# One layer of a conformer and mLSTM hybrid on one core: the order of a head's small matrix products, updates and copies is changed

## What is computed

```python
u = u_a * sigmoid(u_g)
c = conv_general_dilated(concat(conv_buf, u), w_dw, ...) + b_dw      # 31 taps, depthwise
# mLSTM, for each head, chunk by chunk
s = einsum('bthk,bshk->btsh', qc, kc) * w_intra
num = einsum('btsh,bshv->bthv', s, vc) + w_inter * einsum('bhvk,bthk->bthv', C, qc)
den = sum(s, axis=2) + w_inter * einsum('bhk,bthk->bth', n, qc)
h = num / maximum(abs(den), exp(-m_t))
C_new = dec * C + einsum('bsh,bshv,bshk->bhvk', wk, vc, kc)
n_new = dec * n + einsum('bsh,bshk->bhk', wk, kc)
hm = h * rsqrt(mean(h * h) + EPS) * g_mh * sigmoid(o)
```

## Time and profile before

| | us |
|---|---|
| median of 3 runs | 1351.9 (1348.71 to 1354.8) |
| the profiled execution: its own time | 1349.91 |
| its span in the profile | 1348.2 |
| TensorE busy (matmul) | 1272.1, 94% |
| TensorE weight loads (beside the matmuls) | 1184.2, 88% |
| VectorE busy | 734.4, 54% |
| ScalarE busy | 485.3, 36% |
| GpSimd busy | 81.6, 6% |
| mean granted TensorE clock | 0.976 |

### The profile page before, as it was taken

How to read it: one execution, slowest core, us unless ns; L and a number is a source line. 1 busy time by engine, 2 the same in 40 slices (tenths; PEclk the granted TensorE clock), 3 DMA queues, 4 the chain that set the end, 5 groups by cost and what they waited for, 6 DMA issues and landing times.

```text
span 1348.2 us, 23801 instructions
## 1 busy us (share of the span) xinstructions
PE 1272.1 (94%) x9123; PEld 1184.2 (88%) x9123; DVE 734.4 (54%) x994; ACT 485.3 (36%) x701; POOL 81.6 (6%) x139
## 2 busy tenths in 40 slices
PE   6999998999899899989999999995999999999994
PEld 5999967987697688669999999994999999999993
DVE  4343688787888877785455533435644212444324
ACT  6333531452344145314574322235433212333111
POOL 3011101101100110010000000002000000000002
PEclk8999999999999999999999999997999999999997
DMA  5235725505441541341322222330222222222211
GB/s 185 79 117 157 100 88 179 182 31 183 154 141 47 186 182 62 124 156 49 110 79 94 87 86 93 124 114 16 79 93 79 94 93 78 94 78 94 94 47 66
DMA packets 39777, 141.31 MB, mean 105 GB/s; under 512 B 5012, under 2 KB 5524, under 8 KB 39592
## 3 DMA queue, kind: packets, MB, share of 16 engines
q1 hardware_dynamic: 27848, 99.37, 23.0%
q0 software_dynamic: 11872, 41.23, 9.1%
HBM read 118.31 MB, written 22.26 MB: 104 GB/s over the span
## 4 chain that ended last, share of the span: by engine, by line
PE 81%; DVE 8%; issue 6%; ACT 2%; DMA 1%; DVEq 1%; POOL 0%; ACTq 0%; POOLq 0%; SPq 0%
PE product L1254 78%; PE side L1254 3%; DVE accp L962 3%; DVE y L1198 1%; DMA wraw<-in_wstream 1%; DVE wlo L811 1%; DVE crg L1068 1%; DVE accs L975 0%; ACT L667 0%; DMA x<-in_xT 0%; ACT fr L518 0%; DVE pt L1059 0%; ACT L529 0%; DVEq L961 0%; PE side L1391 0%
## 5 line engine op out<-in xcount | busy, mean ns | idle before, releaser
L1254 PE MATMUL product<-ahi,whi 128*128 128x256 f32 (+1 forms) x1536 | 325.0, 293 | 19.0 <-DVE alo L836 10.8
L811 DVE TENSOR_TENSOR wlo<-wraw,whi 128x1024 fp32r<-128x1024 f32 x176 | 214.8, 1223 | 232.4 <-ACT whi L510 224.1
L1254 PE MATMUL product<-ahi,wlo 128*128 128x256 f32 (+1 forms) x1536 | 321.5, 291 | 0.0
L1254 PE MATMUL product<-alo,whi 128*128 128x256 f32 (+1 forms) x1536 | 319.6, 290 | 0.0
L1254 PEld LDWEIGHTS product<-ahi,whi 128*128 128x128 f32 x1536 | 250.4, 192 | 24.2 <-issue 21.5
L510 ACT ACTIVATE whi<-wraw 128x1024 fp32r<-128x1024 f32 x176 | 185.0, 1052 | 240.1 <-PE product L1254 163.0
L1254 PEld LDWEIGHTS product<-alo,whi 128*128 128x128 f32 x1536 | 250.2, 192 | 0.0
L1254 PEld LDWEIGHTS product<-ahi,wlo 128*128 128x128 f32 x1536 | 249.2, 191 | 0.0
L962 DVE SCALAR_TENSOR_TENSOR accp<-u,wdw,accp 128x512 f32<-128x512 f32 x240 | 163.4, 745 | 0.5
L1254 PE MATMUL product<-hidhi,wlo 128*128 128x256 f32 (+1 forms) x512 | 105.8, 287 | 0.0
L1254 PE MATMUL product<-hidlo,whi 128*128 128x256 f32 (+1 forms) x512 | 105.7, 288 | 0.0
(11 more groups left out here) (249 smaller groups left out, 1638.6 us busy)
## 6 DMA issues: line engine op xcount, KB each, us to landing
wraw<-in_wstream SPq DMA_DIRECT2D x176, 512.0 KB, 3.4
crg<-in_c_in POOLq DMA_DIRECT2D x32, 512.0 KB, 6.1
out_c_s<-crg POOLq DMA_DIRECT2D x32, 512.0 KB, 2.9
hb<-head_rows POOLq DMA_DIRECT2D x4, 580.0 KB, 5.6
x<-in_xT SPq DMA_DIRECT2D x4, 544.0 KB, 5.4
sgm<-in_xT SPq DMA_DIRECT2D x1, 2176.0 KB, 9.1
out_yT<-y SPq DMA_DIRECT2D x8, 272.0 KB, 2.1
out_c_p<-cst POOLq DMA_DIRECT2D x4, 512.0 KB, 6.8
```

The costliest lines, as they stand in the source:

```text
L811: V.tensor_tensor(wlo[:, k % RING, :, :], wraw[:, k % 2, :, :], whi[:, k % RING, :, :].bitcast(f32), ALU.subtract).then_inc(lo_done, 1)
L1254: return pe.matmul(out, lhsT, rhs, start=start, stop=stop, skip_group_check=check)
```

## The change

- TensorE: the scores stand behind v2; the denominators (prompt and sample) stand behind v4, ahead of o0; `readout(0)`, cu0 and cu1 behind o0, and the sample's numerator behind them, so that the readout's first matmul starts the accumulation; the sums for n stand behind cu3; the transposes of the sample rows stand behind cc01.
- DVE: the products of the score weights stand behind the drain of v3; the maximum of the denominator stands behind `split(9)`; in the loop over the output gates the state updates and reciprocals stand ahead of the taps; some taps stand among the pv drains (`PV_TAPS`); it no longer computes `kws`, `hs` (twice) and the copies of the convolution into `u`.
- ACT: `kws`, the two rescalings of `hs` and the copies into `u` are added; the sigmoid of a gate chunk stands ahead of the copy of the next weights (`split(11 + k)`); a table for the sigmoid is loaded ahead of o0, and one set for logarithm and exponential behind o3.

```diff
-V_TAPS = [(5, 8), (8, 11), (11, 13), (13, 15)]
-O_TAPS = [(17, 18), (18, 20), (20, 24), (24, 27)]
+V_TAPS = [(5, 8), (8, 11), (11, 13), (13, 13)]
+O_TAPS = [(16, 18), (18, 18), (18, 21), (21, 24)]
+PV_TAPS = [(24, 24), (24, 26), (26, 26), (26, 28)]
...
+                act.wait_ge(bv_in, 16 * h + 16)
+                s = use("kts")
+                act.activation(kws[:, :], psum[s][0:NS, 0, 0:DK], ACT.Copy, scale=wkcol[:, bass.ds(h, 1)]).then_inc(drained[s], 1)
                 was_drained("kts")
...
                 for k in range(VT):
-                    split(11 + k)
+                    if k == 0:
+                        act.activation(warm[:, :], eps[:, :], ACT.Sigmoid).then_inc(table_in, 1)
                     s = use(f"o{k}")
                     act.activation(tile(hm, 4 * h + k), slot(s), ACT.Sigmoid, bias=c("b_o", 4 * h + k)).then_inc(drained[s], 1)
+                    split(11 + k)
+
+                act.preload_act_table_set("natural_log_exp_and_others")
+                act.wait_ge(snum_ready, h + 1)
+                act.wait_ge(srec_ready, h + 1)
+                apart(act)
+                act.activation(hs[:, :], side[:, 3, :], ACT.Copy, scale=sst[:, 1:2]).then_inc(hs_ready, 1)
...
+                act.wait_ge(hs_std, h + 1)
+                act.activation(hs[:, :], hs[:, :], ACT.Copy, scale=sst[:, 4:5]).then_inc(hs_norm, 1)
...
+                act.wait_ge(conv_saved, 16 * 2 * KT)
+                act.wait_ge(conv_sum, 2 * h + 2)
+                apart(act)
+                for q in range(2):
+                    act.activation(tile(u, 2 * h + q, 0, SEQ), accp[:, q:q + 1, :], ACT.Copy).then_inc(conv_copied, 1)
+                    act.activation(tile(u, 2 * h + q, SEQ, NS), accs[:, q:q + 1, :], ACT.Identity, bias=c("b_dw", 2 * h + q)).then_inc(conv_copied, 1)
...
                 for k in range(VT):
                     split(11 + k)
...
                     if k < 2:
                         update(2 * k)
                         update(2 * k + 1)
-                    taps(*O_TAPS[k])
                     if k == 1:
                         dve.wait_ge(dve_step, sd)
+                        V.reciprocal(sst[:, 1:2], sst[:, 0:1]).then_inc(srec_ready, 1)
+                        dve.wait_ge(dve_step, rd)
                         rd = mark(V.reciprocal(rden[:, :], rden[:, :]))
-                        sd = mark(V.reciprocal(sst[:, 1:2], sst[:, 0:1]))
-                dve.wait_ge(snum_ready, h + 1)
-                dve.wait_ge(dve_step, sd)
-                V.tensor_scalar(hs[:, :], side[:, 3, :], sst[:, 1:2], None, ALU.mult).then_inc(hs_ready, 1)
+                    taps(*O_TAPS[k])
...
+                    taps(*PV_TAPS[k])
+                taps(28, WIDTH - 1)
+                taps(WIDTH - 1, WIDTH)
```

More of the change, by code:

```diff
@@ L680, in state_out @@
                                    ACT.Copy).then_inc(drained[s], 1)
+                act.wait_ge(np_ready, h + 1)
+                act.activation(npn[:, bass.ds(h, 1), :], side[:, 2:3, P:P + QT], ACT.Copy).then_inc(np_used, 1)
                 for k in range(VT):
@@ L1033, in _ @@
                     if s_ == 0:
-                        s = use("kts")
-                        V.tensor_scalar(kws[:, :], psum[s][0:NS, 0, 0:DK], wkcol[:, hh], None, ALU.mult).then_inc(drained[s], 1)
                         dve.wait_ge(kh_ready, h + 1)
                         V.tensor_tensor(kwl[:, :], kws[:, :], kwh[:, :].bitcast(f32), ALU.subtract).then_inc(kl_ready, 1)
+                    if s_ == 3:
+                        dve.wait_ge(st_ready, 5 * h + 5)
+                        for q in range(ST + 1):
+                            dve.wait_ge(w_ready, 8 * h + ST + q)
+                            bank, at_ = ST_AT[q]
+                            if q < ST:
+                                w_ = SEQ - P * q
+                                d = pt[:, PT_AT[q]:PT_AT[q] + w_]
+                                V.tensor_tensor(d, d, side[:, bank, at_:at_ + w_], ALU.mult).then_inc(pt_ready, 1)
+                            else:
+                                d = spread(pts[:, :])
+                                V.tensor_tensor(d, d, by_quad(side[0:NS, bank, at_:at_ + NS]), ALU.mult).then_inc(pt_ready, 1)
                     if s_ < 2:
@@ L1049, in _ @@
                 V.tensor_tensor(vst[NS:2 * NS, :], vtok[0:NS, ST, :], vst[0:NS, :].bitcast(f32), ALU.subtract).then_inc(ops_ready, 1)
[L1050 to L1062, removed]
-                split(9)
+                split(9)
+                taps(13, 14)
+                dve.wait_ge(den_abs, h + 1)
+                dve.wait_ge(expm_ready, h + 1)
+                rd = mark(V.tensor_tensor(rden[:, :], rden[:, :], hb[:, R_M:R_M + SEQ], ALU.max))
+                dve.wait_ge(sden_abs, h + 1)
+                sd = mark(V.tensor_tensor(sst[:, 0:1], sst[:, 0:1], mcol[:, hh], ALU.max))
+                taps(14, 16)
                 split(10)
@@ L1368, in values, with scores @@
                     return ins
+                def scores():
+                    pe.wait_ge(kt_used, ST * h + ST)
+                    apart(pe)
+                    for q in range(ST + 1):
+                        bank, at_ = ST_AT[q]
+                        n_, w_ = (P, SEQ - P * q) if q < ST else (NS, NS)
+                        for kk in range(QT):
+                            ins = mm(side[0:n_, bank, at_:at_ + w_], kT[:, kk, P * q:P * q + n_], qT[:, kk, P * q:P * q + w_],
+                                     kk == 0, kk == QT - 1)
+                        ins.then_inc(st_ready, 1)
                 s = use("v0")
@@ new lines, in _ @@
+                for q in range(ST):
+                    ins = mm(side[:, 0, P * q:SEQ], ones[:, :], pt[:, PT_AT[q]:PT_AT[q] + SEQ - P * q], q == 0, q == ST - 1)
+                ins.then_inc(den_ready, 1)
+                pe.wait_ge(ops_ready, 5 * h + 4)
+                mm(side[:, 2, 0:1], pts[:, :], ones[0:NS, 0:1], True, False)
+                for kk in range(QT):
+                    ins = mm(side[:, 2, 0:1], qn[:, kk, :], ones[:, 0:1], False, kk == QT - 1)
+                ins.then_inc(sden_ready, 1)
@@ new lines, in _ @@
+                chunk("o0", 8)
+                readout(0)
+                pe.wait_ge(ops_ready, 5 * h + 5)
+                pe.wait_ge(vs_all, h + 1)
+                pe.wait_ge(kst_ready, 3 * DEC_B * (h + 1))
+                outer(0)
+                outer(1)
+                mm(side[:, 3, :], pts[:, :], vtok[0:NS, ST, :], False, False)
+                chunk("o1", 9)
+                outer(2)
+                outer(3)
+                pe.wait_ge(sden_abs, h + 1)
+                for kk in range(QT):
+                    for q in range(ST):
+                        ins = mm(side[:, 2, P + kk:P + kk + 1], kw[:, q, P * kk:P * (kk + 1)], ones[:, 0:1], q == 0, q == ST - 1)
@@ L1471, in _ @@
+                ins.then_inc(np_ready, 1)
+                chunk("o2", 10)
+                chunk("o3", 11)
                 readout(1).then_inc(snum_ready, 1)
@@ L1494, in _ @@
                 ins.then_inc(hst_ready, 1)
+                outer(6)
+                weighted(2)
+                outer(7)
+                weighted(3)
+                new_state(1)
+                pe.wait_ge(hsum_ready, 3 * h + 3)
+                mm(side[:, 1, :], ones[:, :], sqacc[:, :], True, True).then_inc(ss_ready, 1)
             def alternate(i, k, c0, s0, xhi, xlo, arrive=None):
```

91 lines of the change are left out of this document (21 added, 70 removed).

## The result

The changed kernel takes 1370.0 us (median of 4 runs, 1366.04 to 1374.84) against 1353.4 (1348.71 to 1355.39) of the kernel before: ratio 1.013, 95% interval 1.0084 to 1.0175. It is slower, and outside the range of the prediction. The profiled execution took 1366.04, 16.1 more than that of before (1349.91).

What follows compares the result with a forecast made beforehand. TensorE, busy 94% of the span, was taken as the bound. Waits of +1.35 and clock of -1.5 us a head gave -0.6 over four heads: 1349.3 profiled, 1351.3 from the median 1351.9; range 1346 to 1357, with rivals 1342 to 1360.

Steps and rivals of the forecast that it cites:

- Scores +1.3: Before the scores, now behind v2: a new TensorE wait of 1.3 us a head for ACT's kw.
- o0 +0.85: Before o0: a new wait of 0.85 us a head for DVE's chain behind v3, ending in the weight subtraction.
- cu1 -0.5: Before cu1: its wait goes, as cu0 and the readout lie between; 0.5 us a head saved.
- o1 -1.2, no half clock behind it: Before o1: 0.6 to 0.7 of the 1.84 us wait is left, 1.2 saved, and full clock behind it.
- o2 +0.9, behind ACT's late copy: Before o2: a stall of 1.0 where it had 0.1, as ACT copies the weights after o1's sigmoid.
- 1.27 stays: Before the second readout: the 1.27 us wait for its state loads stays unchanged.
- the stall at cu5 stays too: Before cu5: the 2.35 us wait for DVE to drain cu4 stays, changing by zero.
- The clock, -1.5 a head: Behind cu1, in o1: the half-clock stretch goes, saving 1.5 us a head, bounded at 0 to -1.5.
- Idle time: Over a head: TensorE idle 8 to 9 us instead of 7.
- hs, the conv copies, the sample rows: nothing: Work moved to ACT and later sample-row transposes cost zero; the conv copies have 1.2 us of cover at q0.
- The rival that came true: Smaller but more stalls, at cu3 and o2 and at cu5, bring six more half-clock stretches: +9, 1360.3 us; chance 12%.
- The fourth rival: At cu4: relieved DVE comes sooner, the 2.35 us stall goes with its clock stretches, 1338.9 us; chance 7%.

Runs made afterwards that it cites:

- e9: Kernel before with only ACT's order in the gate steps swapped, sigmoid ahead of the copy of the next weights: 1372.3 us, ratio 1.0133.
- e5: Changed kernel with ACT's gate-step order as before, copy of the next weights ahead of the sigmoid: 1333.3 us, ratio 0.9855.
- e10: Changed kernel with DVE's state updates ahead of the weight subtraction and the sums for n back between pv3 and cc23: 1346.1 us, ratio 0.9946.
- e4: Kernel before with one convolution tap moved from ahead of the updates of cu2 and cu3 to ahead of cu4's: 1361.6 us, ratio 1.0058.
- e6: Kernel before with convolution taps moved from ahead of the updates of cu4 to ahead of those of cu2 and cu3: 1339.8 us, ratio 0.9905.
- e1: Changed kernel with DVE's state updates put ahead of the weight subtraction of each gate step: 1357.2 us, ratio 1.0015.
- e2: Changed kernel with three convolution taps moved from ahead of the update of cu4 to behind the drain of v2: 1342.7 us, ratio 0.992.
- e7: Changed kernel with the scores behind v3 instead of v2: 1358.7 us, ratio 1.0032.
- e3: Changed kernel with DVE's updates ahead of the weight subtraction and three taps moved behind the drain of v2: 1330.7 us, ratio 0.9834.
- e11: Changed kernel with updates ahead of the subtraction, scores behind v3, DVE's sample sums ahead of its score products, some taps earlier: 1322.2 us, ratio 0.9767.

## Why the prediction was wrong, point by point

- **Scores +1.3, o0 +0.85.** Measured 1.23 and 0.63. Right.
- **cu1 -0.5.** Its wait is gone. Right.
- **o1 -1.2, no half clock behind it.** 0.63 is left in three heads, as foretold, and 1.15 in the first; the stretch behind cu1 is gone in those three and has stayed in the first. Right but for the first head, as a local statement.
- **o2 +0.9, behind ACT's late copy.** Measured 0.98 in place of 0.1, with DVE waiting 4.46 for the copy as the step said. e9 and e5 show the cause by adding and removing just that order. Right.
- **"1.27 stays", "the stall at cu5 stays too".** Their sum was right (3.62 foretold, 3.70 measured), the two terms were not. o2 ran at half clock, so its end came 1.6 us later (its sigmoid starts at 348.30, where 340.27, 6.1 for a chunk at full clock and 0.3 to hand over make 346.7), while the loads came no later: the load wait went. In e10, where o2 runs at full clock in every head, each head has a load wait again. The update of cu4 is tied to o3's end by sigmoid, copy, subtraction, six taps; TensorE reached cu5 that much sooner, and the two waits became one of 3.70. The prediction had the coupling only the other way round. Its zero for this part of the head is right all the same, in idle time: 8.13 us from o3's sigmoid to cu5 before, 8.14 after.
- **The clock, -1.5 a head.** This is the step that failed. I took away the stretch behind o1 and left all others where they were, by the size of the single stall. The trace of before already spoke against going by size: the readout of its first head waits 2.12 us, longer than the 1.83 of o1, and the clock stays at its upper level behind it.

```profile
222.06 1.92 PE L1254 MATMUL side<-crg,qm 128*32 128x512 f32 x16 [2.12 <-DMA crg<-in_c_in]
...
222.00:226.00 4.00, 3.94 (x23) 1.00 0.40 130
```

  After the change the stretch that was to be saved came back behind o2 in every head, and the merged stall before cu5 brought one or two in every head instead of two in all: 13 instead of the two that the sum implies. 11 stretches at 1.43 are 15.7 us, most of the 18.7 by which the forecast was low; one of them stands behind the wait in the first head told of below, and is not the change's. From the profiled execution, 1349.3, the forecast was 16.7 low.
- **Idle time.** 8.3 us in the second head, foretold 8 to 9. Over the heads the sum asked for 4 x 1.35 = 5.4 more; measured 9.2 more, 2.6 of it a wait that the profiled execution of before lacks (below).
- **hs, the conv copies, the sample rows: nothing.** No wait of TensorE is put down to them, and DVE's busy time fell from 734.4 to 724.9. e5 bounds them together: the change with ACT's old order is faster than before by 20 us (10.7 from profile to profile). The table load ahead of `hs` takes 1.28 and the next ACTIVATE starts 0.01 behind it, as the earlier trace rows had it. The Trainium skill, "ScalarE: Activation LUTs", "What ACT_TABLE_LOAD costs", counts a drain of about 1.38 us more; this trace shows none either.
- **The rival that came true** is the first one, with its own sign: "It decides if o2 runs at half clock", and "half clock behind cu3 in most heads" stood among the signs of being wrong. It gave 1360.3 and was still too low, since it added six stretches to a sum that had already taken four away. Its chance of 12% rested on a 1.27 us stall that had brought none, and in the kernel after 0.54 and 0.98 with the sums between them did.
- **The fourth rival**, DVE sooner at cu4, was kept down for "the weights' copy behind o3's sigmoid". e5 takes this copy away from there and gets it: the reason was the right one, and it says that the same edit which I priced at +0.9 a head cost the 9 a head (37 / 4; 27 / 4, near 7, from profile to profile) by which e5 is faster. The rival's 1338.9 for the whole is near e5's 1333.3 and 1339.2.

Two of the signs of being wrong came: half clock behind cu3 in all four heads, and heads longer than 123.5 us (124.0 to 127.0 between the first K transposes of one head and of the next). The time by the table: idle +9.2 and seven stretches, 10.0, make 19.2, and 3.1 less in the rest; measured 16.1. What stays open is which stalls bring half clock.

## What to carry to other kernels

Where one engine copies and another works behind that copy in order, the place of the copy in the first one's queue sets all that is queued in the second: ask not only who waits for the copy, but what stands behind the one who waits, here two updates and six taps that TensorE needed. Of two waits that hang on one chain, don't carry the sizes over: fix the chain's end, then see when the waiting engine gets there; a slower TensorE ahead of that end costs nothing, as e10's readout shows. And when stalls become smaller but stay, don't book the clock as won: count where the stretches at half clock were, price them from the rows, and keep their return as a rival of real weight.

## What the runs showed of the hardware

- A stretch at half clock cost 1.30 to 1.43 us of TensorE's busy time on average, with 14 to 30 of them a program. It costs no time where TensorE would have waited anyway (e10's readout).
- No size of a stall separates those with half clock from those without. The 1.83 before o1 brought it in every head of before, but the same wait of 1.83 or 1.84 at the same place in three heads of e4 and in two of e6 only. The 2.14 before e10's readout did, the 2.12 in the first head of before and the 2.50 in the first head of e6, both before the readout, didn't, nor did the 1.27. The 0.54 before cu3 with the one-column sums behind it brought it in every head of after, e1, e2 and e7 (in all of them but e1 a wait before o2 follows), in three heads of e5, and in one each of e3 and e11.
- In the first head TensorE waits 1.5 to 4.0 us in the second half of v0 for weights whose load came late, in the profile of every kernel but the kernel before, also in those of e4, e6 and e9, which are edits of it. The timeline of TensorE in the kernel after has it:

```profile
155.74 0.39 PE L1267 MATMUL product<-whi,ahi 128*128 128x256 f32 x1 [2.64 <-DVE wlo L830]
```

The edits of e4, e6 and e9 stand behind this place in the program, so the wait is no part of the change; whether the executions of before that were not profiled have it is not shown. The profiled execution of before, without it, was 3.4 us below the median of its kernel (1353.35), that of after 4.0 below its own. Of the 16.1 between the two profiles 2.64 are this wait, with what it does to the clock on top.
